# Latent attention: the values of the head behind directly behind the scores, the next head's transposes after them

## The chip, the cores and the metric

The kernel runs on one core of one Trainium2 chip. The metric is the device time of one execution in microseconds; the time of a kernel is the median of its runs. The core's engines work side by side and are ordered by semaphores alone: TensorE (PE in the profile, with its weight loads as PEld) multiplies, ScalarE (ACT), VectorE (DVE) and GpSimd (POOL) work on the elements, SyncE (SP) issues the loads of the weights. Each engine takes its own instructions in the order in which they are written, so a wait in front of one instruction holds all that stand behind it.

## The reference, cut to what matters

A stack of two small transformer blocks on 512 tokens of width 1024. The change touches one stage of it, the latent attention (`mla_layer`): 16 heads of 64 + 32 columns for queries and keys, 64 columns of values, causal softmax:

```python
q = rmsnorm(q, q_head_g); k = rmsnorm(k, k_head_g)          # per head, 96 columns, then rope on 32 of them
logits = jnp.einsum('bhqd,bhkd->bhqk', qi, k) * scale       # scores
w = jax.nn.softmax(jnp.where(mask, logits, -jnp.inf), axis=-1)
o = jnp.einsum('bhqk,bhkd->bhqd', w.astype(v.dtype), v)     # values
o = o.reshape(B, S, MIX_WIDTH) * jax.nn.silu(gate)
return x + o @ w_out
```

Behind it come a gate with the per-layer input, the stick-breaking attention, the gated MLP and the windowed attention, all of which are left as they are.

## The kernel before

All 512 tokens are on the chip at once, as four blocks of 128 queries. Products that need full precision are made of parts: a number is split into a rounded high part and the rest (`w_hi`, `w_lo`, `prT_h`, `prT_l`), and three or two products of the parts are summed in a PSUM bank.

The stage that changes is a loop over 16 heads, written out (`mla_step(h, ...)` on TensorE, `mla_step(h)` on ScalarE and VectorE). I call one turn a step; in step h stand the scores of head h, the transposes of head h + 1 and the values of head h - 1, so the values run one step behind. The order on each engine is that of the code; nothing schedules it anew.

TensorE, step h, before: `mla_scores(h)` (L666, L668: four blocks, with the causal mask added by a product), `mla_q(h + 1)` (L645: four transposes of the next query into bank 6), six products of the gate (`mla_gate_tile`, L479 to L481; in the last pair of heads `out_tile` takes their place), `mla_k(h + 1)` (L645, bank 6 again), six more products of the gate, `mla_values(h - 1)` (L693, L694: eight products into bank 6), `mla_probs_T(h)` (L679: ten transposes of the probabilities into banks 3 to 5).

ScalarE, step h, before: `probs_T(h - 1)` (L1303: three copies of the transposed probabilities to their high parts), `probs(h)` (L1295: four exponentials, with `head_T` of the query, L1277, behind the first of them), `head_T` of the key (L1277), in even steps a weight slab's high part (L1077) and a tanh (L1313), in odd ones `o_hi` (L1307), then `mla_part(h - 1)` (L1332: half of the values' bank is copied out), `mla_v(h + 1)` (L1322).

VectorE, step h, before: `maxima(h)` (L1893, L1887: four row maxima and their scalings, which the exponentials need), `probs_T(h - 1)` (L1914: three subtractions that make the low parts `prT_l`, which the values need), `normalize(h)` (L1904, L1907: reciprocal and four scalings of the probabilities), a slab's low part (L1638) or `mla_gate_read` (L1933) and `o_lo` (L1926), then `mla_sum(h - 1)` (L1939: reads the other half of the values' bank and adds it; its semaphore `o_read` says that bank 6 is free again).

GpSimd turns the heads three ahead (`mla_head`, L2349 to L2352), makes the low part of v (L2366), multiplies the gate (`mla_gated`, L2376) and finishes the silu (L2358, L2359).

Bank 6 thus serves the query's transposes, the key's transposes and the values in turn. Who writes it waits for the one who read the last content: `mla_q` for `kT_ok` and `o_read`, `mla_k` for `qT_ok`, `mla_values` for `kT_ok`.

Of the kernel before, what the change touches and what calls it, by code (L numbers as in the profile page):

```python
# [17 lines left out]
HEADS = 16  # L18
# [96 lines left out]
def build(nc, ctx, ins, out, cols):  # L115
    sems = {}

    def S(name):
        if name not in sems:
            sems[name] = ctx.enter_context(nc.semaphore(name))  # L120
        return sems[name]
# [47 lines left out]
    def put(name, shape, kb, dt=F32, of=None):  # L169

        off = (R2 if of is None else of) + int(kb * 1024)
        assert of is not None or off + int(np.prod(shape[1:])) * 4 <= R2 + R2_SIZE, name
        return nc.alloc_sbuf_tensor_at(name, shape, dt, offset=off)
# [23 lines left out]
    qT = [put(f"qT{s}", [P, T], 10 + 2 * s) for s in range(2)]  # L197
# [200 lines left out]
    def result_bank(m, half):  # L398

        return ps[4 * ((lin["b_out"].group0 + half) % 2) + m]  # L400
# [75 lines left out]
    def _(pe):  # L476
# [165 lines left out]
        def to_T(s, ring, sem, bank=6):  # L642

            for m in range(MB):
                t = pe.transpose(ps[bank][0:QK, m * P:(m + 1) * P], ring[s][:, m, :], ident)  # L645
            t.then_inc(S(sem), 1)

        def mla_q(h, s):
            pe.wait_ge(S("qk_ring"), 2 * h + 2)
            pe.wait_ge(S("kT_ok"), h)  # L650
            if h > 2:
                pe.wait_ge(S("o_read"), h - 2)
            to_T(s, q_ring, "qT_done")

        def mla_k(h, s):
            pe.wait_ge(S("qT_ok"), h + 1)
            to_T(s, k_ring, "kT_done")

        def mla_scores(h, s, first):
            pe.wait_ge(S("kT_ok"), h + 1)  # L660
            if not first:
                pe.wait_ge(S("exp_done"), MB * h)
            for j in reversed(range(MB)):
                b, c = QRY_BANK[j]
                n = (j + 1) * P
                pe.matmul(ps[b][:, c:c + n], qT[s][0:QK, j * P:(j + 1) * P], kT[s][0:QK, 0:n],  # L666
                          start=j != 0, stop=False, skip_group_check=True)
                pe.matmul(ps[b][:, c + j * P:c + n], ident_r[:, :], causal_r[:, :], start=False, stop=True, skip_group_check=True)\  # L668
                    .then_inc(S("s_done"), 1)
# [13 lines left out]
        def mla_values(h, first):  # L683
            pe.wait_ge(S("pT_a"), 3 * h + 3)
            pe.wait_ge(S("pT_b"), 3 * h + 3)
            pe.wait_ge(S("v_ok"), h + 1)
            pe.wait_ge(S("v_lo"), h + 1)
            pe.wait_ge(S("kT_ok"), min(h + 3, HEADS))
            if not first:
                pe.wait_ge(S("o_read"), h)  # L690
            for j in range(MB):
                at = slice(KEY_COL[j], KEY_COL[j] + T - j * P)
                pe.matmul(ps[6][:, j * P:T], v_hl[h % 2][:, j, :], prT_h[:, at], start=j == 0, stop=False, skip_group_check=True)  # L693
                t = pe.matmul(ps[6][:, j * P:T], v_hl[h % 2][:, j, :], prT_l[:, at], start=False, stop=j == MB - 1, skip_group_check=True)  # L694
            t.then_inc(S("o_done"), 1)
# [22 lines left out]
        def mla_step(h, s, i):  # L718

            first, last = h == 0, h == HEADS - 1  # L720
            if first:
                pe.wait_ge(S("kv_up_read"), 11)
            mla_scores(h, s, first)
            if first:
                pe.wait_ge(S(group_read[G + 3][0]), group_read[G + 3][1])
            if not last:
                mla_q(h + 1, 1 - s)
            if i < PAIRS - 1:
                mla_gate_tile(lin["mla_gate1"], i, 7, 4 * s, 4 * s + 2)
            else:  # L730
                out_tile(0, 4 * s, 4 * s + 2)
            if not last:
                mla_k(h + 1, 1 - s)
            if i < PAIRS - 1:
                mla_gate_tile(lin["mla_gate1"], i, 7, 4 * s + 2, 4 * s + 4)
            elif s == 0:
                out_tile(0, 2, 4)
            if not first:
                mla_values(h - 1, h == 1)
            mla_probs_T(h, first)  # L740


# [293 lines left out]
        for k in range(KD):  # L1036
# [4 lines left out]
            if k == 5:  # L1041


                for n, (sem, count, t) in enumerate((("acc_done", 7 * 4 + 6, acc), ("sq_done", 8 * 4 + 8, sq[1]))):
                    pe.wait_ge(S(sem), count)
                    for m in range(MB):
                        last = pe.matmul(result_bank(3, 1)[:, T - MB + m:T - MB + m + 1], t[:, m * P:(m + 1) * P], ones[:, 0:1],
                                         start=n == m == 0, stop=n == 1, skip_group_check=True)
# [8 lines left out]
    def _(act):  # L1057
# [215 lines left out]
        def head_T(h, s, sem, to, g, ok, bank=6):  # L1273
            act.wait_ge(S(sem), h + 1)
            if not (isinstance(h, int) and h < 2):
                act.wait_ge(S("s_done"), MB * (h - 1))
            act.activation(to[s][0:QK, :], ps[bank][0:QK, :], ACT.Identity, scale=gain(g, 0, QK)).then_inc(S(ok), 1)  # L1277
# [7 lines left out]
        def probs(h, s, between=None):  # L1285
            if h:
                act.wait_ge(S("pT_done"), h)
            for r, j in enumerate(reversed(range(MB))):
                if r == 1 and between:
                    between()  # L1290
                act.wait_ge(S("nb_done"), MB * h + (r + 1 if j > 1 else MB))
                b, c = QRY_BANK[j]
                n = (j + 1) * P
                scale = q_ss[:, h, j:j + 1] if isinstance(h, int) else q_ss[:, bass.ds(h, 1), j]
                act.activation(pr[:, QRY_COL[j]:QRY_COL[j] + n], ps[b][:, c:c + n], ACT.Exp, bias=nb[:, j:j + 1],  # L1295
                               scale=scale, accum_out=ssum[:, j:j + 1]).then_inc(S("exp_done"), 1)
# [27 lines left out]
        def mla_part(h):  # L1324

            act.wait_ge(S("o_done"), h + 1)
            if h > 1:
                act.wait_ge(S("o_gated"), h - 1)
            else:
                act.wait_ge(S("qk_ring"), 8)  # L1330
            s = h % 2
            act.activation(o_part[head_rows(s), :, :], ps[6][head_rows(s, True), :].rearrange("p (m t) -> p m t", m=MB), ACT.Copy)\  # L1332
               .then_inc(S("o_part"), 1)

        def mla_step(h):
            i, s = h // 2, h % 2
            more = h < HEADS - 1
            if h:
                probs_T(h - 1)
            probs(h, s, (lambda: head_T(h + 1, 1 - s, "qT_done", qT, "q", "qT_ok")) if more else None)  # L1340
            if more:
                head_T(h + 1, 1 - s, "kT_done", kT, "k", "kT_ok")
            if h == 0:
                k_squares(lin["kv_up"].n - 1)
                mla_v(0)
            if s == 0:
                split_to(lin["mla_gate1"].load0 + i + 1)
            if s == 0 and i:
                mla_tanh(i)
            if s and i:  # L1350
                o_hi(i - 1, o_mh, "o_gated", "o_mla")
            if h:
                mla_part(h - 1)
            if more:
                mla_v(h + 1)

# [264 lines left out]
    def _(dve):  # L1621
# [4 lines left out]
        def split_to(r, i=None):  # L1626

            while ahead[0] <= r:
                split(ahead[0], i)
                ahead[0] += 1  # L1630
# [271 lines left out]
        def normalize(h):  # L1902
            dve.wait_ge(S("exp_done"), MB * h + MB)
            link(dve.reciprocal(rsum, ssum))  # L1904
            for j in reversed(range(MB)):
                at = slice(QRY_COL[j], QRY_COL[j] + (j + 1) * P)
                dve.tensor_scalar(pr[:, at], pr[:, at], rsum[:, j:j + 1], None, ALU.mult).then_inc(S("p_ready"), 1)  # L1907
# [27 lines left out]
        def mla_sum(h):  # L1935

            rows = head_rows(h % 2)
            dve.wait_ge(S("o_part"), h + 1)
            dve.tensor_tensor(o_part[rows, :, :], ps[6][rows, :].rearrange("p (m t) -> p m t", m=MB), o_part[rows, :, :], ALU.add)\  # L1939
               .then_inc(S("o_read"), 1)  # L1940

        def mla_step(h):
            i, s = h // 2, h % 2
            maxima(h)
            if h:
                probs_T(h - 1)
            if h == 1:
                split_to(lin["mla_gate1"].load0 + 1)
            normalize(h)
            if h == 0:  # L1950
                head_sums(k_ss, 4 * HD, "k")(lin["kv_up"], G, MB - 1, None)
            if s == 0 and i:
                split_to(lin["mla_gate1"].load0 + i + 1)
            if s and i < PAIRS - 1:
                mla_gate_read(i + 1)
            if s and i:
                o_lo(i - 1, o_mh, o_ml, "o_mla")
            if h:
                mla_sum(h - 1)

        for h in range(HEADS):
            mla_step(h)
# [614 lines left out]
```

## Time and profile before

| | us |
|---|---|
| median of 3 runs (1332.79 to 1333.91) | 1333.89 |
| the profiled execution | 1334.08 |
| its span, first to last instruction | 1332.3 |
| what lies around the span | 1.8 |
| TensorE busy in the span | 1302.3 (98%) |
| VectorE, ScalarE, GpSimd busy | 769.3, 645.5, 343.4 |
| the 16 heads of latent attention, from the first scores | 116.5 to about 257 |

A busy share is an average over stages of very different kind. TensorE's 98% says that nearly all that is added in front of one of its instructions is added to the time, unless the wait falls where TensorE waits already.

### The profile page before, as it was taken

What the parts mean: (1) busy time and instruction counts of PE and PEld (TensorE: products, weight loads), DVE (VectorE), ACT (ScalarE), POOL (GpSimd) and SP (SyncE); (2) the same over time, 40 slices, a digit from 0 to 9 for tenths busy, and PEclk for the clock granted to TensorE, in tenths of its full rate; (3) what the DMA queues carried; (4) which work ended last, traced back from release to release, by engine and by line L of the source; (5) the groups of instructions that cost most, each with busy time, mean ns of one, the idle gap of its engine ahead of it and who ended that gap; (6) DMA issues with size and microseconds to landing.
All of it is one profiled execution on the core that took longest, in us unless ns stands there. A gap on an engine that the chain in (4) does not pass through costs nothing.

```text
span 1332.3 us, 17876 instructions
## 1 busy us (share of the span) xinstructions
PE 1302.3 (98%) x6494; PEld 1089.4 (82%) x6494; DVE 769.3 (58%) x1207; ACT 645.5 (48%) x1161; POOL 343.4 (26%) x389
## 2 busy tenths in 40 slices
PE   7999999899999999999999999999999999999997
PEld 6997787778888888888888878888888888889876
DVE  5646999744752236898444643336467336578734
ACT  5379887633532325998243423424334224356534
POOL 2238877400000007773000000000000000768520
PEclk9999999999999999999999999999999999999999
DMA  5332111022222232001323323331333331411111
GB/s 191 85 106 68 41 32 32 17 95 95 95 95 95 95 96 79 16 0 32 111 95 95 95 83 103 99 95 51 96 95 106 116 102 50 127 41 40 48 48 64
DMA packets 75811, 104.14 MB, mean 78 GB/s; under 512 B 3428, under 2 KB 37464, under 8 KB 75608
## 3 DMA queue, kind: packets, MB, share of 16 engines
q1 hardware_dynamic: 74672, 99.44, 23.6%
q0 software_dynamic: 944, 3.65, 0.9%
q8 instruction: 47, 0.77, 0.2%
q14 instruction: 28, 0.23, 0.1%
q10 hardware_dynamic: 120, 0.05, 0.0%
HBM read 101.03 MB, written 2.10 MB: 77 GB/s over the span
## 4 chain that ended last, share of the span: by engine, by line
PE 88%; DVE 6%; ACT 3%; issue 2%; DMA 0%; POOL 0%; POOLq 0%; DVEq 0%; SPq 0%; ACTq 0%
PE ps L479 23%; PE ps L481 23%; PE ps L480 23%; PE ps L666 2%; PE ps L969 2%; PE ps L825 2%; PE ps L679 1%; PE ps L815 1%; PE ps L913 1%; PE ps L816 1%; PE ps L693 1%; PE ps L645 1%; DVE sp L2027 1%; PE ps L694 1%; DVE w_lo L1638 1%
## 5 line engine op out<-in xcount | busy, mean ns | idle before, releaser
L1638 DVE TENSOR_TENSOR w_lo<-stage,w_hi 128x1024 fp32r<-128x1024 f32 (+4 forms) x188 | 224.2, 1193 | 402.8 <-ACT w_hi L1077 402.7
L1077 ACT ACTIVATE w_hi<-stage 128x1024 fp32r<-128x1024 f32 (+4 forms) x188 | 191.8, 1020 | 464.3 <-PE ps L481 463.8
L479 PE MATMUL ps<-a0h,w_hi 128*128 128x512 f32 x512 | 204.6, 400 | 0.9 <-DVE q_lo L2205 0.9
L481 PE MATMUL ps<-a0h,w_lo 128*128 128x512 f32 x512 | 200.0, 391 | 0.0
L480 PE MATMUL ps<-a0l,w_hi 128*128 128x512 f32 x512 | 199.5, 390 | 0.0
L2295 POOL TENSOR_TENSOR small<-small 128x16 f32<-128x16 f32 (+2 forms) x15 | 33.5, 2233 | 439.7 <-DVE small L1716 334.6
L479 PE MATMUL ps<-w_hi,a0h 128*128 128x512 f32 (+1 forms) x320 | 122.3, 382 | 0.1
L481 PE MATMUL ps<-w_hi,a0l 128*128 128x512 f32 (+1 forms) x320 | 119.9, 375 | 0.0
L480 PE MATMUL ps<-w_lo,a0h 128*128 128x512 f32 (+1 forms) x320 | 119.8, 374 | 0.0
L481 PEld LDWEIGHTS ps<-a0h,w_lo 128*128 128x128 f32 x512 | 96.1, 188 | 20.7
L479 PEld LDWEIGHTS ps<-a0h,w_hi 128*128 128x128 f32 x512 | 96.2, 188 | 20.1 <-issue 1.3
L480 PEld LDWEIGHTS ps<-a0l,w_hi 128*128 128x128 f32 x512 | 96.3, 188 | 18.3 <-issue 0.2
L479 PE MATMUL ps<-a1h,w_hi 128*128 128x512 f32 x256 | 99.9, 390 | 0.3 <-DVE w_lo L1638 0.3
L481 PE MATMUL ps<-a1h,w_lo 128*128 128x512 f32 x256 | 99.6, 389 | 0.0
L480 PE MATMUL ps<-a1l,w_hi 128*128 128x512 f32 x256 | 99.6, 389 | 0.0
L479 PEld LDWEIGHTS ps<-w_hi,a0h 128*128 128x128 f32 x320 | 60.1, 188 | 11.8 <-issue 1.0
L480 PEld LDWEIGHTS ps<-w_lo,a0h 128*128 128x128 f32 x320 | 60.1, 188 | 10.9 <-issue 1.0
L481 PEld LDWEIGHTS ps<-w_hi,a0l 128*128 128x128 f32 x320 | 60.1, 188 | 10.0
L479 PEld LDWEIGHTS ps<-a1h,w_hi 128*128 128x128 f32 x256 | 48.1, 188 | 10.7 <-DVE w_lo L1638 0.8
L481 PEld LDWEIGHTS ps<-a1h,w_lo 128*128 128x128 f32 x256 | 48.1, 188 | 10.0
L480 PEld LDWEIGHTS ps<-a1l,w_hi 128*128 128x128 f32 x256 | 48.1, 188 | 9.9
L479 PE MATMUL ps<-yh,w_hi 128*128 128x512 f32 x128 | 49.9, 390 | 0.0
(319 smaller groups left out, 2860.7 us busy)
## 6 DMA issues: line engine op xcount, KB each, us to landing
stage<-in_a_w_in SPq DMA_DIRECT2D x48, 512.0 KB, 3.7
stage<-in_ple_w_gate SPq DMA_DIRECT2D x16, 512.0 KB, 3.3
stage<-in_w_kv_shared SPq DMA_DIRECT2D x16, 512.0 KB, 3.5
stage<-in_sb_w_in SPq DMA_DIRECT2D x16, 512.0 KB, 3.7
stage<-in_a_w_out SPq DMA_DIRECT2D x16, 512.0 KB, 3.3
stage<-in_b_w_in SPq DMA_DIRECT2D x16, 512.0 KB, 3.7
stage<-in_mla_w_in SPq DMA_DIRECT2D x8, 512.0 KB, 3.9
stage<-in_mla_w_out SPq DMA_DIRECT2D x8, 512.0 KB, 3.8
```

The source lines that it names most:

```text
L479: pe.matmul(bank, wh, mh, start=start, stop=False)
L480: pe.matmul(bank, wh, ml, start=False, stop=False)
L481: return pe.matmul(bank, wl, mh, start=False, stop=stop)
L645: t = pe.transpose(ps[bank][0:QK, m * P:(m + 1) * P], ring[s][:, m, :], ident)
L666: pe.matmul(ps[b][:, c:c + n], qT[s][0:QK, j * P:(j + 1) * P], kT[s][0:QK, 0:n], start=j != 0, stop=False, skip_group_check=True)
L679: t = pe.transpose(ps[3 + b][:, c + (q - j) * P:c + (q - j + 1) * P], pr[:, QRY_COL[q] + j * P:QRY_COL[q] + (j + 1) * P], ident)
L693: pe.matmul(ps[6][:, j * P:T], v_hl[h % 2][:, j, :], prT_h[:, at], start=j == 0, stop=False, skip_group_check=True)
L825: t = pe.matmul(ps[6 + s][:, j * P:T], v_pair2[:, j, :], a_T[s][:, KEY_COL[j]:KEY_COL[j] + T - j * P], start=j == 0, stop=j == MB - 1, ski ...
L969: t = pe.matmul(ps[W_OUT][:, j * P:j * P + n], v_dup[:, e, j, :], pwT[s][:, j, 0:n], start=j == 0, stop=j == MB - 1, skip_group_check=True)
L1077: act.activation(slab(w_hi[r % 2], L, nk, w), slab(stage[r % 4], L, nk, w), ACT.Copy).then_inc(S("hi_ready"), 1)
L1638: dve.tensor_tensor(slab(w_lo[r % 2], L, nk, w), slab(stage[r % 4], L, nk, w), slab(w_hi[r % 2], L, nk, w), ALU.subtract)\
L2295: return pool.tensor_tensor(ap, ap, minus_half[:, 0:n], ALU.pow).then_inc(S(ready), 1)
```

## The change

In each step of the latent attention the same instructions stand in another order, on three engines.

- TensorE: the values of head h - 1 come directly behind the scores of head h; then the gate's first six products, the query's transposes, the other six, the key's transposes, the transposes of the probabilities.
- TensorE's waits: the query's transposes wait in `o_read` for the sum of the values of head h - 1, which have just been multiplied, where they waited for those of head h - 2; the values wait for the key of head h, no longer for that of head h + 1.
- ScalarE: `mla_part(h - 1)` moves from near the end of the step to behind the first exponential; `head_T` of the query moves from there to behind the last.
- VectorE: `mla_sum(h - 1)` moves from the end of the step to between the three subtractions and the normalization.

```diff
@@ mla_q (TensorE) @@
-            if h > 2:
-                pe.wait_ge(S("o_read"), h - 2)
+            if h > 1:
+                pe.wait_ge(S("o_read"), h - 1)
@@ mla_values (TensorE) @@
-            pe.wait_ge(S("kT_ok"), min(h + 3, HEADS))
+            pe.wait_ge(S("kT_ok"), min(h + 2, HEADS))
@@ mla_step (TensorE) @@
             mla_scores(h, s, first)
-            if not last:
-                mla_q(h + 1, 1 - s)
+            if not first:
+                mla_values(h - 1, h == 1)
             if i < PAIRS - 1:
                 mla_gate_tile(lin["mla_gate1"], i, 7, 4 * s, 4 * s + 2)
             else:
                 out_tile(0, 4 * s, 4 * s + 2)
             if not last:
-                mla_k(h + 1, 1 - s)
+                mla_q(h + 1, 1 - s)
             if i < PAIRS - 1:
                 mla_gate_tile(lin["mla_gate1"], i, 7, 4 * s + 2, 4 * s + 4)
             elif s == 0:
                 out_tile(0, 2, 4)
-            if not first:
-                mla_values(h - 1, h == 1)
+            if not last:
+                mla_k(h + 1, 1 - s)
             mla_probs_T(h, first)
@@ mla_step (ScalarE) @@
-            probs(h, s, (lambda: head_T(h + 1, 1 - s, "qT_done", qT, "q", "qT_ok")) if more else None)
+            probs(h, s, (lambda: mla_part(h - 1)) if h else None)
             if more:
+                head_T(h + 1, 1 - s, "qT_done", qT, "q", "qT_ok")
                 head_T(h + 1, 1 - s, "kT_done", kT, "k", "kT_ok")
@@
-            if h:
-                mla_part(h - 1)
@@ mla_step (VectorE) @@
+            if h:
+                mla_sum(h - 1)
             normalize(h)
@@
-            if h:
-                mla_sum(h - 1)
```

TensorE, step 1, from the end of the scores, before. `q_ring` and `k_ring` are the next head's query and key, `a0h`, `a0l`, `w_hi`, `w_lo` the gate's operands, `prT_h`, `prT_l` the probabilities of head 0, `pr` those of head 1:

```order
L668 MATMUL ps<-causal_r,ident_r 128x128
L645 MATMUL ps<-cst,q_ring_111 96x128 x4
L479 MATMUL ps<-a0h,w_hi_52 128x512
...
L645 MATMUL ps<-cst,k_ring_113 96x128 x4
L479 MATMUL ps<-a0h,w_hi_52 128x512
...
L693 MATMUL ps<-prT_h,v_hl_110 128x512
L694 MATMUL ps<-prT_l,v_hl_110 128x512
...
L679 MATMUL ps<-cst,pr 128x128 x10
```

The same place after the change:

```order
L668 MATMUL ps<-causal_r,ident_r 128x128
L693 MATMUL ps<-prT_h,v_hl_110 128x512
L694 MATMUL ps<-prT_l,v_hl_110 128x512
...
L479 MATMUL ps<-a0h,w_hi_52 128x512
...
L645 MATMUL ps<-cst,q_ring_111 96x128 x4
L479 MATMUL ps<-a0h,w_hi_52 128x512
...
L645 MATMUL ps<-cst,k_ring_113 96x128 x4
L679 MATMUL ps<-cst,pr 128x128 x10
```

The eight products of the values have moved up past both transposes and all twelve products of the gate.

ScalarE, step 1, from the first exponential (`q_tok` is where the part of the values goes, L1332):

```order
 L1295 ACTIVATE pr,small<-ps,small 128x512
+L1332 ACTIVATE q_tok<-ps 64x4x128
+L1295 ACTIVATE pr,small<-ps,small 128x384
+L1295 ACTIVATE pr,small<-ps,small 128x256
+L1295 ACTIVATE pr,small<-ps,small 128x128
 L1277 ACTIVATE qT_105<-ps,gains 96x512
-L1295 ACTIVATE pr,small<-ps,small 128x384
-L1295 ACTIVATE pr,small<-ps,small 128x256
-L1295 ACTIVATE pr,small<-ps,small 128x128
 L1277 ACTIVATE kT_107<-ps,gains 96x512
-L1332 ACTIVATE q_tok<-ps 64x4x128
 L1322 ACTIVATE v_hl_110<-kv_tok 128x4x64
```

Three exponentials now stand behind the copy that waits for the values.

VectorE, step 3, from the first maximum, before:

```order
L1893 TENSOR_REDUCE small<-ps 128x1
L1887 SCALAR_TENSOR_TENSOR small<-small 128x1
...
L1914 TENSOR_TENSOR prT_l<-ps,prT_h 128x512
L1914 TENSOR_TENSOR prT_l<-ps,prT_h 128x384 x2
L1904 RECIPROCAL small<-small 128x4
L1907 TENSOR_SCALAR pr<-pr,small 128x512
...
L1933 SCALAR_TENSOR_TENSOR sgm_63<-ps,rstd 128x512
L1926 TENSOR_TENSOR o_m<-tmp_61,o_m 128x512
L1939 TENSOR_TENSOR q_tok<-ps,q_tok 64x4x128
```

and after it (the same lines of code have a number one lower in the changed kernel):

```order
L1892 TENSOR_REDUCE small<-ps 128x1
L1886 SCALAR_TENSOR_TENSOR small<-small 128x1
...
L1913 TENSOR_TENSOR prT_l<-ps,prT_h 128x512
L1913 TENSOR_TENSOR prT_l<-ps,prT_h 128x384 x2
L1938 TENSOR_TENSOR q_tok<-ps,q_tok 64x4x128
L1903 RECIPROCAL small<-small 128x4
L1906 TENSOR_SCALAR pr<-pr,small 128x512
...
L1932 SCALAR_TENSOR_TENSOR sgm_63<-ps,rstd 128x512
L1925 TENSOR_TENSOR o_m<-tmp_61,o_m 128x512
```

The sum has moved up in front of the normalization; the maxima stand where they stood, in front of the subtractions.

## Rows read from the trace of the kernel before

**Rows 1.** Page, part 1: busy us (share of the span) and instructions, by engine.

```profile
PE 1302.3 (98%) x6494; PEld 1089.4 (82%) x6494; DVE 769.3 (58%) x1207; ACT 645.5 (48%) x1161; POOL 343.4 (26%) x389
```

**Rows 2.** Chain of work, stretch of the heads: start, us, what; steps 2, 9, 15 begin.

```profile
133.39 0.86 PE ps L666 x2
...
195.16 0.86 PE ps L666 x2
...
197.72 0.44 PE ps L645 x4
...
199.56 0.44 PE ps L645 x4
...
201.41 0.47 PE ps L693
...
202.87 1.11 PE ps L679 x10
...
248.33 0.86 PE ps L666 x2
```

**Rows 3.** Timeline, VectorE, steps 8 and 9: start, us, what, [idle before <-releaser].

```profile
187.66 0.67 DVE L1893 TENSOR_REDUCE small<-ps 128x1 f32<-128x512 f32 x1
...
190.55 1.61 DVE L1914 TENSOR_TENSOR prT_l<-ps,prT_h 128x512 fp32r<-128x512 f32 x3
...
196.12 0.69 DVE L1893 TENSOR_REDUCE small<-ps 128x1 f32<-128x512 f32 x1 [0.70 <-PE ps L668]
...
198.77 1.61 DVE L1914 TENSOR_TENSOR prT_l<-ps,prT_h 128x512 fp32r<-128x512 f32 x3
```

**Rows 4.** Timeline, ScalarE, VectorE and a weight load, steps 8 and 9.

```profile
187.06 0.67 DVE L1939 TENSOR_TENSOR q_tok<-ps,q_tok 64x512 f32<-64x512 f32 x1
...
198.85 0.66 ACT L1295 ACTIVATE pr<-ps,small 128x384 f32<-128x384 f32 x1
...
200.47 0.69 ACT L1277 ACTIVATE kT<-ps,gains 96x512 f32<-96x512 f32 x1
...
200.62 0.18 DVE L1904 RECIPROCAL small<-small 128x4 f32<-128x4 f32 x1 [0.24 <-ACT pr L1295]
...
201.38 0.19 PEld L693 LDWEIGHTS ps<-prT_h,v_hl 128*128 128x128 f32 x1 [0.43 <-issue]
...
202.91 0.60 ACT L1332 ACTIVATE q_tok<-ps 64x512 f32<-64x512 f32 x1 [0.56 <-PE ps L694]
```

**Rows 5.** Timeline, step 15: the values wait with no key in front of them.

```profile
252.59 1.61 DVE L1914 TENSOR_TENSOR prT_l<-ps,prT_h 128x512 fp32r<-128x512 f32 x3
...
254.30 0.47 PE L693 MATMUL ps<-prT_h,v_hl 128*128 128x512 f32 x1 [1.97 <-issue]
254.31 1.27 DVE L1907 TENSOR_SCALAR pr<-pr,small 128x512 f32<-128x512 f32 x4
```

**Rows 6.** Timeline, steps 0 and 1.

```profile
122.66 1.15 ACT L1265 ACTIVATE sq_tok<-kv_tok 128x512 f32<-128x512 f32 x2
...
123.84 1.22 DVE L1865 TENSOR_REDUCE small<-sq_tok 128x16 f32<-128x1024 f32 x1
...
128.15 1.62 DVE L1914 TENSOR_TENSOR prT_l<-ps,prT_h 128x512 fp32r<-128x512 f32 x3
```

**Rows 7.** Timeline, TensorE, after the last head: two gaps.

```profile
265.06 0.50 PE L479 MATMUL ps<-o_m,w_hi 128*128 128x512 f32 x1 [1.42 <-DVE o_m L1926]
...
268.51 0.50 PE L479 MATMUL ps<-o_m,w_hi 128*128 128x512 f32 x1 [1.77 <-DVE w_lo L1638]
```

**Rows 8.** Windows: stretch, us, busy of PE, PEld, DVE, ACT, POOL, granted clock, DMA share, GB/s.

```profile
252.00:254.30 2.30, 0.33 (x3) 0.03 (x1) 2.28 (x6) 2.19 (x7) 0.58 (x1) 1.00 0.02 4
...
269.50:270.00 0.50, 0.50 (x3) 0.42 (x2) 0.50 (x1) 0.22 (x1) 0.00 (x0) 0.84 0.45 97
...
271.00:272.00 1.00, 1.00 (x4) 0.81 (x3) 0.00 (x0) 0.00 (x0) 0.00 (x0) 0.50 0.86 227
...
273.00:274.00 1.00, 1.00 (x5) 0.77 (x5) 0.00 (x0) 0.00 (x0) 0.00 (x0) 0.87 0.70 212
```

## The prediction, made before the changed kernel was run

> **What bounds the kernel now.** The page's first part comes first: TensorE is busy for 98% of the span [rows 1]. That is an average, so the chain of work through the sixteen heads is read next [rows 2]. In step 9 every piece of it is TensorE's: the scores start at 195.16, the query's transposes at 197.72 (2.56 us later), the key's at 199.56, the values at 201.41, the transposes of the probabilities at 202.87, and those last 1.11, to 203.98. The pieces are 2.56, 1.84, 1.85, 1.46 and 1.11 us, together 8.82. Both 1.84 and 1.85 are four transposes (0.44) and six products of the gate (1.40), so nothing is lost between them. From step 2 (133.39) to step 15 (248.33) thirteen steps take 114.94 us, 8.84 each. TensorE bounds the stage, and every microsecond for which it waits in a step is paid in full.
>
> Next the timeline of VectorE, for when its results are there [rows 3]. In step 9 the first maximum starts at 196.12, 0.96 after the first score; it had waited 0.70 for TensorE, so it can't start sooner. The low parts of head 8's probabilities (L1914) start at 198.77, 2.65 later, and take 1.61: they are ready at 200.38, **5.22 us after the step began**. TensorE asks for them at 6.25 (201.41), so they are never late. In step 8 VectorE has the previous sum in front, and maxima take 2.89 (187.66 to 190.55). The twelve gate products and the eight transposes between scores and values, 3.69 us of work, are what covers VectorE's maxima and subtractions.
>
> **The values go directly behind the scores.** They are asked for at 2.56 and need `prT_l`, which VectorE still makes behind the maxima, which in turn need the scores of the same step. No wait was added; an old one has lost its cover. Step 15 shows the price without any key in front: the subtractions end at 252.59 + 1.61 = 254.20, and TensorE, which had waited 1.97 us, begins the values at 254.30, 0.10 later [rows 5]. The sum for a middle step:
> - ready at 0.96 + 2.65 + 1.61 + 0.10 = 5.32 us by step 9, and 0.96 + 2.89 + 1.61 + 0.10 = 5.56 by step 8; step 15 itself gives 5.97 (254.30 - 248.33). I take the mean of the first two, 5.44, since the difference is between even and odd steps. TensorE stands still for 5.44 - 2.56 = 2.88 us;
> - values 1.46, to 6.90.
>
> **What follows the values.** The gate's six products (1.40) run to 8.30. Meanwhile the bank must be read for the query: ScalarE's part 0.60, VectorE's sum 0.67 [rows 4], and 0.04, 0.03 and 0.10 for the handovers, 1.44 in all, so the query's transposes start at 8.34. This wait is new, the sum has moved past five instructions of the normalization and a slab's subtraction, and what hides it is the gate's six products; without them it would cost the 1.44. Query 0.44 (8.78), gate 1.40 (10.18), key 0.44 (10.62), probabilities 1.11: **11.73 us**.
> - Is ScalarE in time for the key? It waits in the middle of the softmax for the values: the part ends at 7.54, the other three exponentials and their sums take 1.62 until the next activation (198.85 to 200.47), so the query's copy starts at 9.2 and is done at 9.9. From such a copy's end to TensorE's load it took 0.22 (200.47 + 0.69 = 201.16, load at 201.38) [rows 4]. 10.1 is just before 10.18.
> - Is VectorE? The reciprocal starts 1.77 after those exponentials began (198.85 to 200.62), at 9.35, takes 0.18, and the four scalings 1.27 [rows 5]: all done at 10.8, the first sooner. Transposes from 10.62 to 11.73 just hold, since the last needs the last scaling.
> - Is the next score? The key's copy runs from 10.66 to 11.35, plus 0.22: 11.57, before 11.73.
>
> So TensorE's own work is still the longer line, but ScalarE's and VectorE's are within 0.1 to 0.3 of it. Each middle step costs 11.73 - 8.84 = 2.89 more, the stall itself; thirteen of them **37.6**.
>
> **The ends of the stage.** In step 0 no values exist, but the query's copy has moved behind all exponentials. The key's transposes wait for it, the key's copy ends about 123.7, and the squares behind it on ScalarE start there and not at 122.66, 1.08 later. VectorE's reduction of them (123.84) stands in front of step 1's maxima, so L1914 ends at 128.15 + 1.62 + 1.08 = 130.85 [rows 6], the values start at 130.95, and step 2, 11.73 - 5.44 = 6.29 after that, at 137.24 where it was 133.39: **3.9**. Step 15: values at 5.56 to 7.02, part to 7.66, reciprocal at 9.43, scalings done at about 10.9, the last transpose at about 11.2; before, the transposes ended at 254.30 + 1.46 + 1.11 - 248.33 = 8.54. **2.7**. Nothing moves on SP or in the DMA queues: the weight loads follow the slabs' use, which comes later, not earlier. GpSimd's order is untouched too, and it gets more time per head.
>
> Together 37.6 + 3.9 + 2.7 = 44.2 us. On the profiled execution's 1334.08 that is **1378.3** with TensorE's clock as it is; the median of the runs is 0.2 below that execution, which I leave out.
>
> **The clock.** A stop of 2.9 us in every 11.7 has no match in this trace, so its price has two ends. The granted clock stayed at 1.00 through step 15's stop of 1.97 us [rows 5, 8]. It fell when two stops, 1.42 and 1.77 us, lay within five microseconds with work between [rows 7]: the window from 269.50 shows 0.84, the one at 271.00 shows 0.50 (1.2 of 2.4 GHz), that at 273.00 shows 0.87, so it was low for some 3.4 us [rows 8]. 3.4 us at half clock lose about 1.6 us of work; products of the values, gate and transposes follow a stall directly, and all of them are on the line that bounds. Ends: no fall, nothing; a fall in each of fifteen steps, 23 us. Our stop is longer than the 1.97 that passed and nearly as long as the 3.19 in two pieces that did not. I take a fall in ten of fifteen steps, 10 x 1.55 = **15.5**, and get 1378.3 + 15.5 = 1393.8, rounded to **1393**.
>
> The Trainium skill, "TensorE: Matmul & The Clock Gate", section "Why this matters for your kernels", advises against idle gaps over about 3 us between bursts. By that rule our gap would be just short of trouble and the clock would stay up; the trace's fall after two gaps, each well under that, speaks against taking it as the limit. That is the second rival.
>
> **The rivals.**
> - *Stall with falls of the clock* (the forecast): 1385 to 1402.
> - *Stall, clock stays up*: the middle steps as above, 1378; 1374 if all steps are like step 9 (13 x 0.12 = 1.6 less) and step 0 costs little, 1383 if GpSimd's work holds small VectorE instructions as in step 15 (5.97 for 5.56).
> - *ScalarE's half of the softmax becomes the bound.* Three exponentials behind the part leave 0.1 to 0.3 us of room. If falls of the clock in the scores and GpSimd's interference come together, the key or the probabilities' transposes wait some 0.5 us more a step: 15 x 0.5 = 7.5, from 1402 up to 1410.
> - *The stall is partly hidden*: were `prT_l` ready some 1.5 us sooner, because the maxima are quick behind a free VectorE, 15 x 1.4 = 21 less: 1357. Rows 3 speak against it: in step 9 VectorE was already idle and waiting for the first score.
> - *Not slower*: the values no longer wait for the next key. Its place is the load of their weights, which sat idle for 0.43 us in step 9 [rows 4], though the chain shows only 0.01 of it; with step 15's 1.97 the gain would be 2 to 3 us, 1331. It decides only where `prT_l` is ready within 2.56 us of a step's start, and the rows have 5.22.
> - *The change doesn't do what it says*: the order on each engine shows that it does, and no scheduler stands between.
>
> **How the numbers follow.** Forecast with falls 0.56; clock stays up 0.31; ScalarE's side on top 0.07; partly hidden 0.04; not slower 0.02. The likeliest is 1393. The range must take in the case with the clock up, so it goes from 1374 to 1404: that leaves out the partly hidden, the not slower and most of the case above. A measurement of this kernel can tell about 0.2% (2.7 us) from no change; all but the last case are far beyond: slower 0.98, within 0.2% 0.01, faster 0.01.
>
> **What the changed profile would show.** Right: in steps 2 to 14 TensorE's first product of L693 has about 2.9 us of idle time in front, and VectorE's subtractions are what ended it; a step takes 11.7 us with the clock at 1.00 and up to 13.3 in those with a low stretch; no idle time in front of L645's query (0.1 at most) or L679; the granted clock dips between 130 and 320; all behind the stage takes as long as before. Wrong: an idle time well below 2.9 (VectorE's line is read wrongly); a step far from 11.7 at full clock (ScalarE's line); a clock of 1.00 throughout (then 1378).

## The result

The changed kernel takes **1415.47 us** (median of 4 runs, 1414.8 to 1415.99) where the kernel before takes 1333.9: a ratio of 1.0613, 95% interval 1.0594 to 1.0631. The prediction was 1393 with a range of 1374 to 1404. The direction and the kind of loss (TensorE waits for the values' operand, and its clock falls behind the waits) were forecast; the size was not. The time lies 11 us above the range, and the loss is 81.6 us where 59 were forecast.

The changed kernel's page, part 1 (busy us, share, instructions) and the granted clock in 40 slices (part 2), against [rows 1]:

```profile
PE 1328.1 (94%) x6494; PEld 1112.5 (79%) x6494; DVE 768.7 (54%) x1207; ACT 646.1 (46%) x1161; POOL 340.0 (24%) x389
...
PEclk9999888889999999999999999999999999999999
```

The same instructions take 26 us more of TensorE's time (the same products at a lower clock) and leave it 55 us more of idle time. Its waits name the place, `PE ps L693`, the first product of the values (us in total, times, longest):

```profile
PE ps L693 <- issue: 57.3, 15, 5.0
```

"Issue" means that the profile names no releaser; the code waits there for several semaphores. The timeline shows which came last. Step 3 of the changed kernel begins at 153.25 (start, us, what, idle time in front); the rows answer to [rows 3] and [rows 4]:

```profile
152.35 0.68 ACT L1277 ACTIVATE kT<-ps,gains 96x512 f32<-96x512 f32 x1 [1.13 <-PE ps L645]
152.94 1.04 ACT L1077 ACTIVATE w_hi<-stage 128x1024 fp32r<-128x1024 f32 x1
...
154.01 1.23 DVE L1637 TENSOR_TENSOR w_lo<-stage,w_hi 128x1024 fp32r<-128x1024 f32 x1 [2.91 <-ACT w_hi L1077]
...
155.27 0.69 DVE L1892 TENSOR_REDUCE small<-ps 128x1 f32<-128x512 f32 x1
...
156.68 1.26 POOL L2358 TENSOR_TENSOR sgm<-tmp,sgm 128x512 f32<-128x512 f32 x1
156.87 1.08 DVE L1886 SCALAR_TENSOR_TENSOR small<-small 128x1 f32<-128x1 f32 x1
...
158.41 1.61 DVE L1913 TENSOR_TENSOR prT_l<-ps,prT_h 128x512 fp32r<-128x512 f32 x3
...
160.12 0.52 PE L693 MATMUL ps<-prT_h,v_hl 128*128 128x512 f32 x1 [4.15 <-issue]
```

The subtractions end at 160.02 and TensorE goes on at 160.12, the handover of 0.10 of [rows 5]: that is the forecast wait, but it is 4.15 us long, not 2.9. The first maximum starts 2.02 us after the step began, because the weight slab's low part (L1637) stands in front of it. Before, in step 9, it was 1.12 (196.12 - 195.00); the 0.96 of the prediction counts from 195.16, where the chain of work puts the same step's start. So it is 0.90 us late. The maxima then take 3.14 us where they took 2.65, 0.49 more: one scaling that works on 128 numbers takes 1.08 us beside a GpSimd operation. The two starts of step 9 before, on the timeline:

```profile
195.00 1.02 PE L666 MATMUL ps<-kT,qT 96*128 96x512 f32 x2
...
196.12 0.69 DVE L1893 TENSOR_REDUCE small<-ps 128x1 f32<-128x512 f32 x1 [0.70 <-PE ps L668]
```

Step 14 lies in the last pair of heads, with no slab in front and no heads left to prepare on GpSimd. Windows of steps 3, 4, 5 and 14 (stretch, us, busy of PE, PEld, DVE, ACT, POOL, granted clock, DMA share, GB/s), and step 14's values:

```profile
153.25:167.77 14.52, 10.37 (x52) 8.52 (x51) 8.76 (x19) 7.59 (x18) 8.73 (x14) 0.88 0.14 36
167.77:181.64 13.87, 10.38 (x52) 8.52 (x51) 7.62 (x18) 6.64 (x17) 4.27 (x8) 0.88 0.00 1
181.64:197.38 15.74, 11.60 (x52) 9.43 (x51) 8.76 (x19) 7.59 (x18) 8.74 (x14) 0.78 0.12 33
313.43:325.15 11.72, 9.00 (x53) 7.10 (x51) 6.97 (x18) 6.53 (x17) 1.99 (x2) 1.00 0.00 0
```

```profile
318.82 0.47 PE L693 MATMUL ps<-prT_h,q_tok_r 128*128 128x512 f32 x1 [2.66 <-issue]
```

Step 14 is nearest to the step of the prediction: 11.72 us where 11.73 was worked out, at a clock of 1.00. The twelve middle steps are not: their waits are 4.14 (odd), 3.50 (even; 3.16 in step 2), and each holds one or two stretches of some 3.4 us at half clock:

```profile
146.00:147.00 1.00, 1.00 (x9) 0.95 (x7) 0.00 (x0) 0.00 (x0) 0.00 (x0) 0.87 0.00 0
147.00:150.00 3.00, 3.00 (x9) 2.28 (x9) 1.04 (x3) 2.34 (x7) 0.00 (x0) 0.50 0.00 0
150.00:151.00 1.00, 1.00 (x7) 0.89 (x6) 1.00 (x4) 0.47 (x1) 0.00 (x0) 0.92 0.00 0
```

A step with one such stretch shows 0.88, one with two 0.78. All time at half clock from the first values on adds up to 64.9 us, 19 stretches of 3.41, where ten had been taken. The last two lie in step 15.

### The profile page after: what moved, and what is told of

Read it like the earlier page. It is cut to its first block, busy times and chain, and to the rows that moved or that the text cites. A ratio compares the mean times of both kernels' runs of the same rounds, so it can differ in the third digit from the quotient of the medians.

```text
span 1413.6 us, 17877 instructions
## 1 busy us (share of the span) xinstructions
PE 1328.1 (94%) x6494; PEld 1112.5 (79%) x6494; DVE 768.7 (54%) x1207; ACT 646.1 (46%) x1161; POOL 340.0 (24%) x389
## 4 chain that ended last, share of the span: by engine, by line
PE 84%; issue 6%; DVE 5%; ACT 4%; DMA 0%; POOL 0%; DVEq 0%; POOLq 0%; ACTq 0%; SPq 0%
PE ps L479 23%; PE ps L480 22%; PE ps L481 22%; PE ps L969 2%; PE ps L825 2%; PE ps L693 1%; PE ps L666 1%; PE ps L694 1%; PE ps L645 1%; PE ps L913 1%; PE ps L815 1%; ACT w_hi L1077 1%; PE ps L816 1%; DVE sp L2026 1%; ACT prT_h L1303 1%
## 5 line engine op out<-in xcount | busy, mean ns | idle before, releaser
L1637 DVE TENSOR_TENSOR w_lo<-stage,w_hi 128x1024 fp32r<-128x1024 f32 (+4 forms) x188 | 224.2, 1192 | 418.9 <-ACT w_hi L1077 418.9
L479 PE MATMUL ps<-a0h,w_hi 128*128 128x512 f32 x512 | 210.4, 411 | 0.8 <-DVE q_lo L2204 0.8
L480 PE MATMUL ps<-a0l,w_hi 128*128 128x512 f32 x512 | 204.2, 399 | 0.0
L481 PE MATMUL ps<-a0h,w_lo 128*128 128x512 f32 x512 | 204.1, 399 | 0.0
L479 PEld LDWEIGHTS ps<-a0h,w_hi 128*128 128x128 f32 x512 | 100.2, 196 | 21.0 <-issue 1.3
L480 PEld LDWEIGHTS ps<-a0l,w_hi 128*128 128x128 f32 x512 | 99.6, 195 | 18.7 <-issue 0.2
L481 PEld LDWEIGHTS ps<-w_hi,a0l 128*128 128x128 f32 x320 | 60.1, 188 | 10.1
```

Of the source, the lines that this page charges most:

```text
L479: pe.matmul(bank, wh, mh, start=start, stop=False)
L480: pe.matmul(bank, wh, ml, start=False, stop=False)
L481: return pe.matmul(bank, wl, mh, start=False, stop=stop)
L1637: dve.tensor_tensor(slab(w_lo[r % 2], L, nk, w), slab(stage[r % 4], L, nk, w), slab(w_hi[r % 2], L, nk, w), ALU.subtract)\
```

## The experiments

Eleven kernels were run. Three things lie on top of each other in the changed kernel: the wait itself, what makes it longer than forecast, and the clock. The first group takes them apart.

**The clock, held up by filling the wait.** Edit on the changed kernel:

```diff
             if not first:
+                for _ in range(12):
+                    pe.matmul(ps[6][:, :], ident_r[:, :], a0h[:, 0, :], start=True, stop=True)
                 mla_values(h - 1, h == 1)
```

> The changed kernel with twelve products of 128x512 (identity times an activation, 0.233 us apart, 2.8 us in all) into bank 6 directly before the values of steps 1 to 15; the values overwrite them, so nothing is computed from them, they only fill the time in which TensorE waits. Theory: in the changed kernel every stall but that of step 14 is followed by one or two stretches of 3.4 us at half clock, 19 in all, each worth about 1.5 us; with the stalls filled the clock stays at 1.00, steps take 13.0 (odd) and 12.3 (even) instead of 14.5 to 15.8 and 13.9, and the time is about 1415 - 19 x 1.5 = 1387. Rival: the steps are long because ScalarE's and VectorE's chain is late, the low clock lies beside it: at most 5 us less, 1410 or more. The wait in front of the values shrinks by 2.8 us in either case, without moving their start.

Measured 1395.11 us, ratio to before 1.0464 (1.0446 to 1.0481), 20.4 us less than the changed kernel. Steps 3, 4 and 14:

```profile
149.05:162.28 13.23, 11.85 (x64) 9.21 (x63) 8.70 (x19) 7.47 (x18) 8.80 (x14) 1.00 0.16 40
162.28:174.88 12.60, 11.86 (x64) 9.21 (x63) 7.66 (x18) 6.51 (x17) 4.31 (x8) 1.00 0.01 1
291.34:303.05 11.71, 11.65 (x65) 9.20 (x64) 6.97 (x18) 6.52 (x17) 1.99 (x2) 1.00 0.01 1
```

The clock stays at 1.00 and the values start where they did (6.90 and 6.26 us into the step), so the fill hardly moved anything else. The theory holds in kind: the low clock costs 20 us, and the rival's 5 at most is out. The theory's size was too large: 28 us at 1.5 a stretch, where 20.4 / 19 = 1.1 was measured.

**The slab out of the way of the maxima.** ScalarE:

```diff
+            def between():
+                if s == 0 and i:
+                    split_to(lin["mla_gate1"].load0 + i + 1)
+                mla_part(h - 1)
-            probs(h, s, (lambda: mla_part(h - 1)) if h else None)
+            probs(h, s, between if h else None)
...
-            if s == 0:
+            if h == 0:
                 split_to(lin["mla_gate1"].load0 + i + 1)
```

and on VectorE the same `split_to` goes from behind `normalize(h)` to in front of `mla_sum(h - 1)`.

> The changed kernel with the weight slab's two halves moved into ScalarE's and VectorE's idle time: ScalarE makes the high part between the first exponential and the copy of the values' part, VectorE the low part between the three subtractions and the sum. Theory: in odd steps the slab's low part (1.23 us) stands in front of the first maximum, which starts at 2.03 instead of 1.12 us; without it the odd steps' wait before the values falls from 4.14 to about 3.1, seven steps by about 1.0, and the time is 7 us less, 1408. Rival: the small scalings of the maxima are held by GpSimd, and that alone makes odd steps late: no more than 2 us less, 1413.

Measured 1402.59 us, ratio 1.0518 (1.05 to 1.0535): 12.9 less, more than forecast. The first maximum of odd steps starts at 1.12 and their wait falls from 4.14 to 2.76, by 1.4 rather than 1.0. The maxima also got faster. The scaling that took 1.08 us takes 0.24: it still ends with GpSimd's operation beside it, but now begins only just before that end. The rest of the 12.9 is clock: 15 stretches at half clock in the stage in place of 19. Where two followed the wait of an odd step, one or none does now, though step 4 has two where it had one. Two odd steps with nearly the same wait (2.78 and 2.76 us) show what a stretch costs, steps 3 and 9:

```profile
153.15:164.96 11.81, 8.98 (x53) 7.09 (x51) 6.69 (x18) 6.53 (x17) 8.32 (x14) 1.00 0.00 0
232.77:245.90 13.13, 10.37 (x53) 8.46 (x52) 6.77 (x18) 6.64 (x17) 8.31 (x14) 0.87 0.01 2
```

They differ by 1.32 us; TensorE is busy for 1.39 us more in the second.

**The tanh moved as well.** One line more in `between`, `mla_tanh(i)` behind `split_to`, and the same line taken out of its old place.

> As e2_slab, and the tanh of the gate is moved to the same idle time of ScalarE, so GpSimd's silu (3.2 us) starts some 6 us sooner, inside the stall and not beside the next step's maxima. Theory: the scaling of 1.08 us in the odd steps' maxima falls to 0.2 to 0.5 and the wait before the values to about 2.7; a further 3 us, 1404. Rival: GpSimd's next piece of work slides into its place and the maxima are held as before: 1408, the same as e2_slab.

Measured 1405.48 us, ratio 1.0541 (1.0523 to 1.0558), 2.9 more than with the slab alone (the single runs do not overlap: 1404.12 to 1406.53 against 1401.31 to 1403.65). The theory fell. The rival, that the next work of GpSimd slides into the gap, is right in kind; the time is slightly worse than it said. In the odd steps the preparation of the next heads now runs beside the maxima, and their wait is 3.16 where it was 2.76. Step 15, which has no heads left to prepare, does gain: its wait falls from 3.64 to 2.56.

**Both causes at once.** The twelve products and the slab's edit together.

> Both e1_fill12 and e2_slab: the clock held up by twelve products that nobody reads, and the slab moved out of the way of the maxima. Theory, the causes add: odd steps from 3 on fall from 13.2 (e1) to 11.8, even ones stay at 12.6, seven times 1.4 less than e1's 1395.1, 1385. Rival: with the clock up the slab is hidden elsewhere: 1392 or more.

Measured 1384.97 us, ratio 1.0381 (1.0364 to 1.0399), as the theory had it: 10.1 less than the fill alone. The odd steps take 11.82 to 11.85, the even ones 12.6 as before.

**GpSimd's part.** On top of that, from head 4 on:

```diff
+            if h < 4:
                 pool.tensor_copy(q_ring[s][:, :, 0:HD], q[:, :, 0:HD])
                 rotate(q_ring[s][:, :, HD:QK], q[:, :, HD:QK], 0, s, "qk_ring")
                 pool.tensor_tensor(k_ring[s][:, :, 0:HD], k, r.to_broadcast([P, MB, HD]), ALU.mult)
+            else:
+                to = q_ring[s][:, :, HD:QK]
+                pool.tensor_tensor(to, to, rope_b[s][:, :, :], ALU.add).then_inc(S("qk_ring"), 1)
```

> e5_fill_slab, and from head 4 on GpSimd leaves out four of its six operations that prepare the next queries and keys (copy, two products of the rotation, scaling of the key), so the heads' queries and keys are wrong, while every semaphore is still raised. Theory: even steps take 12.6 where odd ones take 11.8 because GpSimd's operations hold VectorE's small scalings (0.85 us between the first maximum and the subtractions); with most of them gone all middle steps take 11.7 to 11.9, 5 us less than e5, and with the clock up and the slab away the time is the predicted 1378 plus what step 1 costs, 1380. Rival: the 0.85 us are TensorE's or ScalarE's, and even steps stay at 12.6.

(Left out are five of its seven operations a head, not four of six, so the later heads' queries and keys are not made.) Measured 1380.97 us, ratio 1.035 (1.0333 to 1.0368). Steps 4 and 5:

```profile
161.24:172.96 11.72, 11.66 (x64) 9.18 (x63) 8.11 (x19) 7.47 (x18) 2.04 (x3) 1.00 0.16 46
172.96:184.88 11.92, 11.85 (x65) 9.20 (x63) 6.78 (x18) 6.54 (x17) 6.41 (x8) 1.00 0.00 0
```

The even step falls from 12.60 to 11.72: 0.88 us between its first maximum and its subtractions were GpSimd's. (The odd steps rise a little, from 11.83 to 11.92.) How it looks from VectorE, in the kernel with fill and slab, step 4 (from 162.18):

```profile
163.58 0.61 POOL L2357 TENSOR_TENSOR k_ring<-kv_tok,small 128x256 f32<-128x256 f32 x1
...
164.63 1.28 POOL L2382 TENSOR_TENSOR tmp<-q_tok,sgm 64x512 f32<-64x512 f32 x1
...
165.28 0.65 DVE L1893 SCALAR_TENSOR_TENSOR small<-small 128x1 f32<-128x1 f32 x1
...
165.99 0.73 POOL L2372 TENSOR_TENSOR v_hl<-kv_tok,v_hl 128x256 fp32r<-128x256 f32 x1
166.05 0.75 DVE L1893 SCALAR_TENSOR_TENSOR small<-small 128x1 f32<-128x1 f32 x2
```

Both scalings end as the GpSimd operation beside them ends, or just behind (165.93 and 165.91; 166.80 and 166.72). With 1381 the predicted 1378.3 for a full clock is nearly reached, but with work taken off GpSimd that the changed kernel has to do.

**The same without the fill.**

> e8_fill_slab_pool without its twelve filling products: every step from the second on has the wait that was predicted, 2.7 to 2.9 us, and the clock is free to fall. It measures the clock's term of the sum by itself. The prediction had ten falls worth 15.5 us. Theory now, from the steps of e2_slab that differ in the clock alone (13.13 and 11.81 us at the same wait of 2.76): a fall costs 1.3 us, and nearly every stop of 2.8 us is followed by one, 1381 + 14 x 1.3 = 1399. Rival: falls of this size come only behind stops over 3 us, as the steps 3, 5 and 14 of e2_slab suggest, and only step 1 has one: 1384.

Measured 1395.87 us, ratio 1.0462 (1.0445 to 1.048). Against 1380.97 that is **14.9 us for the clock** where the waits of steps 2 to 14 are near the forecast (2.56 to 2.85 us; 4.16 in step 1, 3.64 in step 15). The prediction's term was 15.5. My newer expectation of 1399 was too much, and the rival's 1384 too little: of steps 2 to 14 nine have a stretch of low clock and four have none; steps 1 and 15 have two each, 13 in all. Steps 6, 7 and 8:

```profile
191.10:202.81 11.71, 8.99 (x52) 7.10 (x51) 8.10 (x19) 7.46 (x18) 2.02 (x3) 1.00 0.15 45
202.81:216.01 13.20, 10.37 (x52) 8.51 (x51) 6.84 (x18) 6.63 (x17) 6.33 (x8) 0.87 0.00 1
216.01:229.07 13.06, 10.40 (x52) 8.36 (x51) 8.10 (x19) 7.57 (x18) 2.02 (x3) 0.87 0.14 40
```

Steps 6 and 8 have the same wait (2.67 and 2.66 us) and the same work, and differ in the clock alone.

**Half the fill.** As the first one with `range(6)`.

> e1_fill12 with six products in place of twelve, so that the changed kernel's waits of 2.7 to 4.1 us shrink by 1.4 to 1.3 to 2.7. It asks whether a stop of that size still lets the clock fall. Theory: with the longest stop at 2.75 us some steps still fall, odd ones above all: 1397 to 1405. Rival: only stops over 2.8 us matter: 1395, as with twelve.

Measured 1408.44 us, ratio 1.0548 (1.0530 to 1.0565). The rival fell and the forecast was low: step 4 stops for 2.08 us only and the clock still falls, while step 13 stops for 2.71 without one (windows of the two):

```profile
163.63:177.53 13.90, 11.82 (x59) 9.50 (x58) 7.66 (x18) 6.64 (x17) 4.30 (x8) 0.88 0.00 1
...
293.89:307.11 13.22, 10.46 (x58) 8.08 (x57) 8.68 (x19) 7.49 (x18) 7.99 (x11) 1.00 0.13 40
```

So the length of the stop does not decide alone whether the clock falls. What else does is left open here.

**The stop in two pieces.** The gate's first six products back between scores and values:

```diff
-            if not first:
-                mla_values(h - 1, h == 1)
             if i < PAIRS - 1:
                 mla_gate_tile(lin["mla_gate1"], i, 7, 4 * s, 4 * s + 2)
             else:
                 out_tile(0, 4 * s, 4 * s + 2)
+            if not first:
+                mla_values(h - 1, h == 1)
```

> The changed kernel with the gate's first six products (1.40 us) moved back between the scores and the values; the values still wait for VectorE's subtractions, and the query's transposes now stand directly behind the values and wait for the sum. Theory: the start of the values stays (5.4 to 6.9 us into the step), the wait before them falls by 1.4 and a new one of 1.4 before the query's transposes takes its place, so at full clock the step is as long as before; what changes is only that the stop is in two pieces with work between, and the clock may fall less: 1390 with no falls, 1415 with all. Rival: the values' position itself costs (their results are later for all behind): then the time falls by 1.4 x 15 = 21 with the clock's pattern unchanged.

Measured 1417.13 us, ratio 1.0621 (1.0595 to 1.0647), level with the changed kernel. The values start at 6.88 in odd steps as before, the wait in front of them is 1.4 shorter (2.71), a new one of 1.5 stands in front of the query, and the clock falls in most steps. The rival fell: putting six products of the gate back in front of the values gives nothing back, since the query's transposes, now directly behind the values, wait for the sum instead. Both waits hang on the subtractions, wherever the gate stands. Cutting the stop in two did not keep the clock up either: there are 20 stretches at half clock.

The second group asks whether the wait is VectorE's order, and whether the idea can be saved.

**The subtractions first.** One exchange on VectorE, on the changed kernel:

```diff
-            maxima(h)
             if h:
                 probs_T(h - 1)
+            maxima(h)
```

> The changed kernel with one thing turned round on VectorE: the three subtractions that make the values' operand stand in front of the maxima, no longer behind them. Theory: the wait in front of the values is VectorE's order and nothing else; the subtractions then wait only for ScalarE's copies (1.33 us from the step's start, later in odd steps, where a slab and a tanh stand in front of them), the values start at about 2.6 in even and 3.4 us in odd steps, the maxima and the softmax come 1 us later, steps take 9.2 to 10, the clock stays up, 1345 us. Rival: the softmax behind the values is the true bound, so the step stays above 11 us and the time above 1365.

Measured 1356.51 us, ratio 1.0161 (1.0144 to 1.0178), **59 us less** by two lines. The theory holds: the values start at 2.62 in even steps, with no wait, and at 3.87 in odd ones, behind a wait of 1.15. The 59 us are wait and clock together: the idle time in front of the values falls from 57.3 to 9.9 us, and of the 19 stretches at half clock in the stage one is left, in step 1. The time comes out 11 above the forecast, since odd steps take 11.1 and not 10 (steps 3 and 4):

```profile
145.31:156.41 11.10, 9.47 (x53) 7.01 (x51) 8.84 (x19) 8.03 (x19) 9.22 (x15) 1.00 0.19 48
156.41:165.82 9.41, 8.90 (x51) 7.11 (x51) 6.96 (x19) 6.09 (x16) 4.16 (x6) 1.00 0.00 0
```

**The slab early as well.** On top of it, ScalarE's `split_to` between the copies of the query and the key.

> e3_sub_first with the slab's high part on ScalarE moved from behind the key's copy to in front of it, where ScalarE waits 1.1 us for TensorE. Theory: in e3 the odd steps (11.1 us, even ones 9.4) are long by the slab, which holds ScalarE's copies of the transposed probabilities and VectorE's first work; with the slab in idle time they fall to about 9.6 and the time to 1356.5 - 7 x 1.5 = 1346. It stays slower than the kernel before, since even the even steps take 9.2 to 9.4 where they took 8.84. Rival: the tanh and the copy of v alone hold the copies as long, 1353 or more.

Measured 1348.57 us, ratio 1.0114 (1.0097 to 1.0131). The odd steps fall to 9.6, the even ones rise to 9.55 and step 1 stays at 12.3. It is still 14 us slower than before. In the middle steps TensorE waits 0.20 us in front of the values and some 0.4 us in front of the query's transposes, in even steps for VectorE's sum:

```profile
158.18 0.47 PE L693 MATMUL ps<-prT_h,q_tok_r 128*128 128x512 f32 x1 [0.20 <-issue]
...
161.44 0.61 PE L645 MATMUL ps<-cst,q_ring 128*96 128x128 f32 x4 [0.36 <-DVE q_tok L1941]
```

The sum follows ScalarE's copy of the values' part, which stands behind the first exponential, and that comes later with the maxima behind the subtractions.

**The kernel before, subtractions first.** The same exchange on the kernel before.

> The kernel before with the subtractions in front of the maxima on VectorE, nothing else. It asks what that order costs where the values stand late. Theory: the operand was 1 us early anyway, so nothing is gained; the softmax comes about 1 us later, the normalization ends at about 8.2 where TensorE transposes the probabilities from 7.9 to 9.0, some 0.1 to 0.3 us lost per step, 1334 to 1338. Rival: the last step's wait of 1.97 us goes and no other wait comes: 1332.

Measured 1348.63 us, ratio 1.011 (1.0093 to 1.0127). Both expectations fell. The last step's wait did go (its values start at 4.0 us with no idle time), but steps 3 to 14 take 9.7 to 9.85 and steps 1 and 2 take 10.5. The first exponential comes 1.0 us later and the query's copy stands behind it on ScalarE, so TensorE waits in front of the key, and another 0.38 in front of the values for the key's copy. I had looked at the normalization and not at that copy:

```profile
199.53 0.64 PE L645 MATMUL ps<-cst,k_ring 128*96 128x128 f32 x4 [0.34 <-ACT qT L1277]
```

So VectorE's order is right for where the values stood before, maxima first because the exponentials are urgent and the values are not, and wrong for where they stand after the change. No version here beats the kernel before.

## Why the prediction was wrong, point by point

- **TensorE bounds the stage, and the values' wait is the price.** Right. 57.3 us of idle time stand in front of L693 in 15 waits, and the exchange of two groups on VectorE took 59 us of time away, the slower clock behind the waits included.
- **The sum of a middle step, 11.73 us.** Right for the step it describes: 11.72 in step 14, 11.68 to 11.92 in steps 2 to 14 once slab and GpSimd are out of the way, and with the clock up 1381 where 1378.3 was worked out. That it fits to 0.01 is luck: the wait is 2.66 and not 2.88, and the chain behind it is as much longer, since the query's transposes take 0.61 us behind a wait and not 0.44. The three conditions on ScalarE and VectorE (key's copy, normalization, next score) held, so the rival that made ScalarE the bound fell too.
- **"The first maximum starts at 0.96".** This is the step that failed: on the timeline's count the first maximum starts at 2.02 in odd steps, where the rows had 1.12. I took the start from [rows 3], where VectorE was waiting for TensorE, and did not ask what would stand in front of it in the new order. The key's transposes now come last on TensorE, so the key's copy comes last on ScalarE, the slab's high part behind it, and its low part (1.23 us) on VectorE after the next scores have begun. I had named the slab where the sum moves past it, and nowhere else. Price: 10.1 us (fill against fill with slab moved): the values of the seven odd steps from 3 to 15 start 1.4 us sooner.
- **Maxima of 2.65 and 2.89.** Mis-sized for the even steps: 3.39 (from 168.89 to 172.28 in step 4). The prediction put the 2.89 of step 8 behind the early start of step 9, and did not ask why it was longer than 2.65. In step 8 the scalings ended with GpSimd's operations, and they still do after the change (step 8 before, step 4 after):

```profile
188.46 1.27 POOL L2376 TENSOR_TENSOR tmp<-q_tok,sgm 64x512 f32<-64x512 f32 x1
...
189.28 0.47 DVE L1887 SCALAR_TENSOR_TENSOR small<-small 128x1 f32<-128x1 f32 x1
...
189.81 0.74 POOL L2366 TENSOR_TENSOR v_hl<-kv_tok,v_hl 128x256 fp32r<-128x256 f32 x1
189.87 0.76 DVE L1887 SCALAR_TENSOR_TENSOR small<-small 128x1 f32<-128x1 f32 x2
```

```profile
171.55 0.72 POOL L2365 TENSOR_TENSOR v_hl<-kv_tok,v_hl 128x256 fp32r<-128x256 f32 x1
171.62 0.74 DVE L1886 SCALAR_TENSOR_TENSOR small<-small 128x1 f32<-128x1 f32 x2
```

  An earlier start of the maxima (1.12 us into the step, not 1.48) therefore did not bring an earlier end: the subtractions start at 4.51, where they started at 4.37. Without most of GpSimd's preparation they start at 3.67. Price: 4.0 us.
- **The ends, 3.9 and 2.7.** The first is right: with the clock up step 1 takes 13.2 where it took 9.1, 4.1 more, and step 0 takes 0.1 less. The 2.7 for step 15 was too small: its wait is 5.02 us, and the last head's transposes start 13.61 us into the step where they started at 7.42. The runs show why. With the slab moved the wait is 3.64, with the tanh moved as well 2.56, and then those transposes start at 10.07, 2.65 later than before, where 2.7 was forecast.
- **The clock's term: 15.5.** Right in sum for the waits that were forecast (14.9), by two errors that cancel: 13 stretches of some 1.15 us, not ten of 1.55. Nothing in the rows had given the number ten, and their own working gave 1.6 and not 1.55. For the longer waits there are 19, and it is 20.4.
- **The sum of the misses:** from the unrounded 1393.8 to 1415.5 it is 21.7 us. Slab 10.1, GpSimd 4.0, 2.7 left at full clock, 4.9 more clock. It closes because each is a difference between two runs; the 2.7 was not traced further.
- **The range.** Its upper end, 1404, left room for more falls of the clock and a little interference. None of the rivals had the waits longer than rows 3 and 5 showed, except GpSimd's 5.97 for 5.56. The rival "clock stays up" failed: falls followed stops of 2.08 to 2.7 us. The Trainium skill, "TensorE: Matmul & The Clock Gate", section "Why this matters for your kernels", warns of idle gaps over about 3 us; taken as a limit below which the clock stays up, it does not hold here.

## What to carry to other kernels

Work that is moved up to where its operand is not ready costs the difference in full on the bounding engine, so look first at which engine makes the operand and what stands in front of it there: here two groups exchanged on VectorE were worth 59 of 82 us. When the last instruction of a step changes on one engine, follow everything that it releases on the others into the next step: each of those may now stand in front of the first urgent instruction there. When two numbers come from different steps (a start from one, a duration from another), ask whether the same work on a third engine sets the end of both. And price a stop in a bounding TensorE with the slower clock behind it, here 15 us on 43 of idle time and 20 on 57.

## What the runs showed of the hardware that was not expected

- The granted clock fell from 1.00 to 0.50 behind stops of 2.08 us (even steps with half the fill) and did not fall behind some of 2.56 to 2.78 us in otherwise equal steps. Each low stretch lasted 3.41 us, or twice that, and cost 1.1 to 1.35 us of time, less than the 1.55 that the times from product to product give (0.43 us in the changed kernel from 148.37 on, against 0.23).
- A VectorE scaling of 128 numbers takes 0.16 us alone and up to 1.08 us beside a GpSimd operation, and then ends within 0.1 us of it. The three subtractions from PSUM kept their length (1.60 to 1.62 us) beside GpSimd in the steps read here.
